# Expert rows added in memory by the DMA, and the attention's value product in two column halves

## What is computed

```python
out = jnp.einsum('bkgnqs,bnskd->bnqkgd', p.astype(v.dtype), vv)      # 8 heads share 2 value heads of 64
...
def hierarchical_moe(xn, ...):
    # every token picks TOP_K = 2 of 32 experts; gates = softmax over the two, times the group's weight
    order = jnp.argsort(expert_idx)                       # 2048 assignments, sorted by expert
    padded = (counts + 128 - 1) // 128 * 128              # each expert's rows are padded to blocks of 128
    x_pad = zeros.at[dest].set(xt[token_idx[order]])
    def expert_block(args):
        hb = jax.nn.silu(xb @ w_g[e]) * (xb @ w_u[e])     # 1024 -> 512
        return hb @ w_d[e]                                # 512 -> 1024
    y = y_pad[dest] * gates[order][:, None]
    out = zeros.at[token_idx[order]].add(y)
...
x = x + hierarchical_moe(rms_norm(x, norm_ffn), ...)
return rms_norm(x, norm_final)
```

## Time and profile before

| | us |
|---|---|
| median of 3 runs | 2939.61 |
| the runs | 2932.75 to 2940.99 |
| the profiled execution, its own time | 2939.56 |
| its span in the profile | 2937.8 |
| TensorE busy | 2763.1 (94%) |
| mean granted TensorE clock | 0.972 |

### The profile page before, as it was taken

How to read it: one execution, slowest core, us unless ns; L and a number is a source line. 1 busy time by engine, 2 the same in 40 slices (tenths; PEclk the granted TensorE clock), 3 DMA queues, 4 the chain that set the end, 5 groups by cost and what they waited for, 6 DMA issues and landing times. The chain is left out here.

```text
span 2937.8 us, 38551 instructions
## 1 busy us (share of the span) xinstructions
PE 2763.1 (94%) x14688; PEld 2408.4 (82%) x14688; DVE 1679.8 (57%) x2116; ACT 1179.0 (40%) x1703; POOL 514.7 (18%) x299
## 2 busy tenths in 40 slices
PE   8989999999899999999998998889999899999993
PEld 7989999899789999988776888666777588888883
DVE  5356655462443343343434732674444899999997
ACT  4342333421311111122334212564433377777774
POOL 3000000002022122100110000002610144444441
PEclk9999999999999999999999999999999899999997
DMA  5342323343211111113313121112302599999996
GB/s 193 103 135 84 99 86 109 119 141 115 86 51 44 49 50 43 50 50 108 134 65 108 44 60 63 37 51 94 108 24 110 185 414 418 414 413 417 413 414 250
DMA packets 244300, 436.95 MB, mean 149 GB/s; under 512 B 21698, under 2 KB 180690, under 8 KB 218594
## 3 DMA queue, kind: packets, MB, share of 16 engines
q1 hardware_dynamic: 234690, 400.88, 37.8%
q0 software_dynamic: 9504, 34.61, 2.9%
HBM read 375.54 MB, written 59.90 MB: 148 GB/s over the span
## 5 line engine op out<-in xcount | busy, mean ns | idle before, releaser
L3547 DVE TENSOR_TENSOR k_w_lo<-k_raw,k_w_hi 128x2048 fp32r<-128x2048 f32 x192 | 433.6, 2289 | 34.4 <-ACT k_w_hi L3483 31.0
L3483 ACT CAST k_w_hi<-k_raw 128x2048 fp32r<-128x2048 f32 x192 | 363.0, 1911 | 64.7 <-PE bank L3401 41.7
L120 PE MATMUL bank<-u_ffn_hi,f_w_hi 128*128 128x342 f32 (+1 forms) x840 | 292.3, 348 | 5.6 <-POOL f_w_lo L1362 5.6
L122 PE MATMUL bank<-u_ffn_hi,f_w_lo 128*128 128x342 f32 (+1 forms) x840 | 293.0, 349 | 0.0
L121 PE MATMUL bank<-u_ffn_lo,f_w_hi 128*128 128x342 f32 (+1 forms) x840 | 292.9, 349 | 0.0
L120 PE MATMUL bank<-u_hi,p_w_hi 128*128 128x342 f32 (+2 forms) x720 | 238.2, 331 | 8.9 <-DVEq L889 6.0
L121 PE MATMUL bank<-u_lo,p_w_hi 128*128 128x342 f32 (+2 forms) x720 | 232.4, 323 | 0.0
L122 PE MATMUL bank<-u_hi,p_w_lo 128*128 128x342 f32 (+2 forms) x720 | 231.9, 322 | 0.0
L3399 PE MATMUL bank<-k_w_hi,k_x_hi 128*128 128x512 f32 x512 | 203.1, 397 | 1.2 <-DVE k_x_lo L3553 1.0
L3401 PE MATMUL bank<-k_w_hi,k_x_lo 128*128 128x512 f32 x512 | 199.8, 390 | 0.0
L3400 PE MATMUL bank<-k_w_lo,k_x_hi 128*128 128x512 f32 x512 | 199.4, 389 | 0.0
(11 more groups left out here) (578 smaller groups left out, 6623.0 us busy)
## 6 DMA issues: line engine op xcount, KB each, us to landing
k_raw<-in_w_e_gate_dram SPq DMA_DIRECT2D x64, 1024.0 KB, 7.0
k_raw<-in_w_e_up_dram SPq DMA_DIRECT2D x64, 1024.0 KB, 7.5
k_raw<-in_w_e_down_dram SPq DMA_DIRECT2D x64, 1024.0 KB, 8.0
d_raw<-in_ffn_w_down_dram SPq DMA_DIRECT2D x44, 512.0 KB, 3.4
p_w<-in_w_in_dram SPq DMA_DIRECT2D x34, 512.0 KB, 4.3
f_raw<-in_ffn_w_gate_dram SPq DMA_DIRECT2D x22, 512.0 KB, 3.6
f_raw<-in_ffn_w_up_dram SPq DMA_DIRECT2D x22, 512.0 KB, 3.6
gate_scratch<-g_out SPq DMA_DIRECT2D x20, 513.0 KB, 6.3
```

The source lines that it names most:

```text
L120: pe.matmul(out, wh[:, t, :], xh[t][:, c:c + n], start=t == 0, stop=False)
L122: m = pe.matmul(out, wl[:, t, :], xh[t][:, c:c + n], start=False, stop=t == tiles - 1)
L3483: act.copy(wh[:, q, :], raw[:, r, :]).then_inc(hi_made, 1)
L3547: dve.tensor_tensor(wl[:, q, :], raw[:, r, :], wh[:, q, :], ALU.subtract).then_inc(lo_made, 1)
```

## The change

- `weigh`: no widened copy. Each value head's 64 columns are the weights of products that write to their own half of the output partitions, and products of the two halves now alternate. There are still four products of 512 columns a block, now with 64 weight columns instead of 128. GpSimd's three instructions and their semaphore are gone.
- Router: SyncE also stores the token rows `h` themselves to a new scratch tensor `sum_scratch`, 8 stores of 512 KB in runs of 512 bytes, among the stores of the normed rows. The gates go through the list of rows as a second column group: two more VectorE instructions, products of 96 columns instead of 48, and one more copy to `weight`.
- Experts: `gated` multiplies by the row's gate in the same instruction. The scatter adds its rows to `sum_scratch` in memory (`compute_op=ALU.add`), at the token's row; padding slots go to 128 spare rows. From the third on, gathers take their row numbers from `assigned` with a bound, so that padding slots, whose number is beyond it, are left out.
- End: one load of 512 KB a block, no adding on VectorE, and the norm on whole rows.

```diff
 # stage_mixers
-            pool.memset(vz[:, :, :, :], 0.0).then_inc(v_wide, 1)
-            pool.wait_ge(v_wide, 1)
-            for kv in range(2):
-                half = slice(kv * DH, (kv + 1) * DH)
-                pool.tensor_copy(vz[:, :, kv, half], va[:, :, half]).then_inc(v_wide, 1)
...
             def weigh(n):
-                if n == 0:
-                    pe.wait_ge(v_wide, 3)
                 pe.wait_ge(pt_kept, 4 * n + 4)
-                for kv in range(2):
-                    for r in range(2):
+                for r in range(2):
+                    for kv in range(2):
+                        half = slice(kv * DH, (kv + 1) * DH)
                         probs = pt[:, r, :, :].rearrange("p (g e) t -> p e g t", e=2)[:, kv]
-                        m = pe.matmul(T[1][:, :], vz[:, n + r, kv, :], probs, start=kv == r == 0, stop=kv == r == 1)
+                        m = pe.matmul(T[1][half, :], va[:, n + r, half], probs, start=r == 0, stop=r == 1)
 # stage_route
+            def rows_out(n):
+                sp.wait_ge(x_kept, n + 1)
+                if n in SHARED:
+                    sp.wait_ge(x_half, SHARED.index(n) + 1)
+                sp.dma_start(sum_d[n * P:(n + 1) * P, :].rearrange("p (k t) -> p k t", t=P), rows_of(h, n)).then_inc(h_stored, 16)
             for n in range(NB):
+                if n < NB - 2:
+                    rows_out(n)
+                if n == NB - 3:
+                    rows_out(NB - 2)
+                    rows_out(NB - 1)
                 sp.wait_ge(xn_made, n + 1)
                 sp.dma_start(xn_d[n * P:(n + 1) * P, :], xn[:, n % 4, :]).then_inc(stored[n % 4], 16)
...
+            sp.wait_ge(h_stored, 16 * NB)
...
-                m = pe.matmul(bank[7][:, 0:MAXB], at_place[:, c, :], in_block[:, c, :], start=c == 0, stop=c == 2 * NB - 1)
+                m = pe.matmul(bank[7][:, 0:2 * MAXB], at_place[:, c, :], in_block[:, c, :, :], start=c == 0, stop=c == 2 * NB - 1)
...
-                then(dve.tensor_tensor(in_block[:, half, :], *marks(begin[:, half], MAXB, begins[:, :]), ALU.is_equal))
-                return dve.tensor_tensor(in_block[:, half, :], in_block[:, half, :], own[:, half].unsqueeze(2).to_broadcast([P, NB, MAXB]), ALU.mult)
+                then(dve.tensor_tensor(in_block[:, half, 0, :], *marks(begin[:, half], MAXB, begins[:, :]), ALU.is_equal))
+                then(dve.tensor_tensor(in_block[:, half, 1, :], in_block[:, half, 0, :], gates[:, half].unsqueeze(2).to_broadcast([P, NB, MAXB]), ALU.mult))
+                return dve.tensor_tensor(in_block[:, half, 0, :], in_block[:, half, 0, :], own[:, half].unsqueeze(2).to_broadcast([P, NB, MAXB]), ALU.mult)
...
+            then(dve.tensor_copy(weight[:, 0:MAXB], bank[7][:, MAXB:2 * MAXB]))
 # stage_experts
+                    d = pool.indirect_dma_start(out=xg[:, s, :], out_offset=None, in_=xn_d, in_offset=rows_at, bounds_check=SEQ - 1, oob_is_err=False)
...
-                pool.indirect_dma_start(out=y_d, out_offset=bass.IndirectOffsetOnAxis(ap=to[:, s:s + 1], axis=0),
-                                        in_=y[:, s, :], in_offset=None).then_inc(stored[s], 16)
+                pool.indirect_dma_start(out=sum_d, out_offset=bass.IndirectOffsetOnAxis(ap=to[:, s:s + 1], axis=0),
+                                        in_=y[:, s, :], in_offset=None, compute_op=ALU.add).then_inc(stored[s], 16)
...
-                dve.tensor_tensor(hb[:, :].rearrange("p (k q) -> p q k", k=KE), sg[:, :].rearrange("p (q k) -> p q k", k=KE),
-                                  bank[3][:, :].rearrange("p (q k) -> p q k", k=KE), ALU.mult).then_inc(hb_made, 1)
+                dve.scalar_tensor_tensor(hb[:, :].rearrange("p (k q) -> p q k", k=KE), sg[:, :].rearrange("p (q k) -> p q k", k=KE), weight[:, ds(b, 1)],
+                                         bank[3][:, :].rearrange("p (q k) -> p q k", k=KE), ALU.mult, ALU.mult).then_inc(hb_made, 1)
...
             for b in range(NB):
-                if b >= RAW:
-                    sp.wait_ge(mixed, b - RAW + 1)
-                for j in range(2):
-                    sp.dma_start(raw[:, b % RAW, j * D:(j + 1) * D], y_d[j * SEQ + b * P:j * SEQ + (b + 1) * P, :]).then_inc(loaded[b % RAW], 16)
+                sp.dma_start(total[:, b, :], sum_d[b * P:(b + 1) * P, :]).then_inc(loaded[b], 16)
...
-                dve.scalar_tensor_tensor(rows_of(h, b), made(0, b), gates[:, b:b + 1], rows_of(h, b), ALU.mult, ALU.add).then_inc(first, 1)
-                dve.wait_ge(first, b + 1)
-                dve.scalar_tensor_tensor(rows_of(h, b), made(1, b), gates[:, NB + b:NB + b + 1], rows_of(h, b), ALU.mult, ALU.add).then_inc(mixed, 1)
-                if b:
-                    norm(b - 1)
-            norm(NB - 1)
```

More of the change, by code:

```diff
@@ L2023, in stage_mixers @@
 def stage_mixers(nc, ctx, A, K, bank, qa, ka, va, qk, vm, og, cols, dist, sinks, rows_d, mk, mv, mem_rows, w_in):
-    (scored, logit, maxed, exped, root, turned, pt_kept, pvmm, small, spread, inverse_kept, scaled, sq_made, sums, logs, rstd_made, placed, v_wide) = sems(
-        ctx, nc, "a", "scored logit maxed exped root turned pt_kept pvmm small spread inverse_kept scaled sq_made sums logs rstd_made placed v_wide")
+    (scored, logit, maxed, exped, root, turned, pt_kept, pvmm, small, spread, inverse_kept, scaled, sq_made, sums, logs, rstd_made, placed) = sems(
+        ctx, nc, "a", "scored logit maxed exped root turned pt_kept pvmm small spread inverse_kept scaled sq_made sums logs rstd_made placed")
     (bc0, bc1, rm_made, dec, gate_made, fmm, s_made, q_made, kt, kw_made, omm, den_made, hmade, umm, state,
@@ L2971, in rows_of, with stage_route @@
     return h[:, :, b * P:(b + 1) * P]
-def stage_route(nc, ctx, A, K, bank, h, gates, assigned, token, table, xn_d, wr, br, gain, raw, pieces_in):
-    (turned, x_kept, x_half, lmm, squared, roots, xn_made, stored_a, stored_b, stored_c, stored_d, rmm, cnt, iotas, rows, act_rows, marked, weighed, listed, lt_kept, l_turned) = sems(
-        ctx, nc, "r", "turned x_kept x_half lmm squared roots xn_made stored_a stored_b stored_c stored_d rmm cnt iotas rows act_rows marked weighed listed lt_kept l_turned")
+def stage_route(nc, ctx, A, K, bank, h, weight, assigned, token, table, xn_d, sum_d, wr, br, gain, raw, pieces_in):
+    (turned, x_kept, x_half, lmm, squared, roots, xn_made, stored_a, stored_b, stored_c, stored_d, rmm, cnt, iotas, rows, act_rows, marked, weighed, listed, lt_kept, l_turned, h_stored) = sems(
+        ctx, nc, "r", "turned x_kept x_half lmm squared roots xn_made stored_a stored_b stored_c stored_d rmm cnt iotas rows act_rows marked weighed listed lt_kept l_turned h_stored")
     ident, ones, eps, lower = (K[n] for n in ("ident", "ones", "eps", "lower"))
@@ L3249, in _ @@
             dve.tensor_copy(table[:, :], tf[:, :])
-            then(dve.memset(assigned[:, MAXB:MAXB + 2], 0))
+            then(dve.memset(assigned[:, MAXB:MAXB + 2], SEQ))
             dve.wait_ge(listed, 1)
@@ L3264, in stage_experts @@
     gathered, stored = (g0, g1), (s0, s1)
-    all_stored, gain_in, first, mixed, squared, normed, out_stored = sems(ctx, nc, "o2", "all_stored gain_in first mixed squared normed out_stored")
-    loaded = sems(ctx, nc, "o2", " ".join(f"in{r}" for r in range(RAW)))
+    all_stored, gain_in, squared, logs, rooted, normed, out_stored = sems(ctx, nc, "o2", "all_stored gain_in squared logs rooted normed out_stored")
+    loaded = sems(ctx, nc, "o2", " ".join(f"in{b}" for b in range(NB)))
     ident, eps = K["ident"], K["eps"]
@@ L3287, in tiles @@
             return ap.rearrange("p (k t) -> p k t", t=P)
[L3289 to L3294, removed]
+        total = h[:, :, :].rearrange("p k t -> p (k t)").rearrange("p (b d) -> p b d", d=D)
         def turn_of(j):
@@ L3343, in index, with gather @@
                 pool.wait_ge(index_made, g)
-            def gather(g, b, s):
-                index(g, from_, s, token, b)
+            def gather(g, b, s, whole=False):
+                index(g, from_, s, token if whole else assigned, b)
                 pool.sem_inc(waited, 1)
                 pool.wait_ge(waited, 1)
-                pool.indirect_dma_start(out=xg[:, s, :], out_offset=None, in_=xn_d,
-                                        in_offset=bass.IndirectOffsetOnAxis(ap=from_[:, s:s + 1], axis=0)).then_inc(gathered[s], 16)
+                rows_at = bass.IndirectOffsetOnAxis(ap=from_[:, s:s + 1], axis=0)
+                if whole:
+                    d = pool.indirect_dma_start(out=xg[:, s, :], out_offset=None, in_=xn_d, in_offset=rows_at)
+                else:
+                    d = pool.indirect_dma_start(out=xg[:, s, :], out_offset=None, in_=xn_d, in_offset=rows_at, bounds_check=SEQ - 1, oob_is_err=False)
+                d.then_inc(gathered[s], 16)
             def scatter(g, b, s):
@@ L3363, in end @@
                 pool.sem_inc(y_stored, 1)
-            gather(1, 0, 0)
-            gather(2, 1, 1)
+            gather(1, 0, 0, True)
+            gather(2, 1, 1, True)
```

(14 more changed lines are left out.)

34 lines of the change are left out of this document (17 added, 17 removed).

## The result

The changed kernel takes 2951.26 us (median of 6 runs, 2949.30 to 2954.14), the kernel before beside it 2940.85. The ratio is 1.0043, with an interval of 1.0025 to 1.0060: **slower**, by about 10 us (0.4%), where I had forecast 16 us less. The profiled execution took 2949.32 us with a span of 2947.6, against 2937.8 of before. I cut both spans at two points: the first row turn of the expert loop (TensorE turns a block's gathered rows) and the last scatter.

What follows compares the result with a forecast made beforehand. The expert loop was taken as bound by TensorE at 17.71 us a period, with DMA nearly touching and taking over after the change. Mixers -15.5, router +2.5, end -16.0, loop +13.4 sum to -15.6: 2924 us from 2939.56, range 2908 to 2952.

Steps and rivals of the forecast that it cites:

- Gathers leave out half of the slots: Expert loop: bounded gathers skip 2048 of 4096 slots, saving 0.64 us of DMA work a period if skipped rows cost nothing.
- case 4: Expert loop: left-out rows still take engine time, adding scatter at two plain ones; loop +32.6 us, total 2943; chance 0.08.
- My own sign of being wrong: Expert loop: main step wrong if the period stays at 17.71 us (near 2910) or exceeds 18.8 (slower than before).
- case 3: Expert loop: the adding scatter costs more than 2.4 plain ones, engines held during the read; at 3, 2962 us; chance 0.20.
- The adding scatter at two plain ones: Expert loop: a scatter that adds takes 2.58 us of DMA time, twice the plain 1.29, so +1.29 a period.
- The DMA work of 17.63 us: Expert loop before the change: DMA engines' work per period, from shrinking landing times, 0.08 us under TensorE's 17.71.
- 13.4: Expert loop: us added over 30 periods, 19.5 of extra DMA work less 6.1 of spare.
- When it sets in: Expert loop: extra DMA work reaches TensorE from about the fifth period, the period then going from 17.7 to 18.2-18.4 us.
- Mixers: `weigh`: passes in alternate column halves pair, 3.5 us becoming 1.75 a block; gain 15.5 us in all, lower end 0.
- Router: Router stage: added VectorE instructions +1.4 us and eight stores +1.1 us, together +2.5 us.
- the stores' term: Router: SyncE's eight added stores delay the stores of normed rows that VectorE waits for, +1.1 us, between 0 and 4.
- The end: After the last scatter: smaller first load, no VectorE adding, ScalarE leading with squares 1.75 us apart; -16.0 us, -12 to -17.

Runs made afterwards that it cites:

- e7: The changed kernel with each expert's rows seated evenly over the partitions instead of filling them from partition 0: 2928.69 us, ratio 0.9963 to the kernel before.
- e8: The changed kernel with the scatter bounded too, leaving out padding rows, and the rows seated evenly over the partitions: 2917.72 us, ratio 0.9934 to the kernel before.
- e2: The changed kernel with a plain scatter in place of the adding one: 2916.61 us, ratio 0.9919 to the kernel before.
- e4: The changed kernel with a bound on the scatter too, so its padding rows are left out: 2942.72 us, ratio 1.0019 to the kernel before.
- e9: The changed kernel with whole gathers and two plain scatters to scratch tensors in place of the adding one: 2944.26 us, ratio 1.0015 to the kernel before.
- e3: The changed kernel with all gathers whole, so padding slots are read as well: 2947.07 us, ratio 1.0023 to the kernel before.

## Why the prediction was wrong

- **The failed step: "Gathers leave out half of the slots: -0.64 us a period, if a left-out row costs nothing."** That left-out rows cost nothing held: e7 shows nearly this saving when it falls evenly (18.57 to 18.00, 0.57). What failed is the unspoken half of the step, that a saving in bytes is a saving on every engine. The rows lie on one side of the partitions, some engines save nothing, and a weight piece waits for those. Instead of -0.64 the term was 19.13 - 18.57 = +0.56, wrong by 1.2 us a period. That it isn't negative is explained by the seats; why it is above zero stays open. My case 4 had the saving at zero for another reason, and with it 2943; a loss was not among my bounds. My own sign of being wrong, a period beyond 18.8, came true.
- **Luck.** 2951 lies just inside my range of 2908 to 2952, but only because the range reached up into case 3, a dearer adding scatter, and that case is false.
- **The adding scatter at two plain ones** was right (18.57 beside 18.58). With this agrees the rule that the Trainium skill (Collectives: The Full Stack, on the bandwidth ceiling of a ring step) states, a reducing step at twice the time of a copying one. Case 3, more than 2.4 plain ones, falls: the outcome lies on its side of the forecast, but not by its mechanism.
- **The DMA work of 17.63 us** was 17.31. I took the fall of the landing times from 9.0 to 7.2 for a queue that was worked off at a steady rate. It was near its floor early: in the same view of before, the up pieces took 7.7 us from 2450 to 2550, 7.5 in the next 100 us, 7.2 after that and 7.2 at the end. Nor did the DMA share of 1.01 say that the engines were full, since e8 has it too, with room to spare. The error in the work hid part of the first one: 17.63 + 1.29 + 0.56 would be 19.48, above the measured 19.13. With 17.31 and even seats the sum is 17.31 - 0.64 + 1.27 = 17.94, close to e7's 18.00. In e7 the stretch from the first row turn to the last scatter took 584.9 us, 8.3 more than before, where I had 13.4.
- **When it sets in:** I expected the fifth block; it was the eleventh to twelfth.
- **Mixers** -15.5 forecast, -11 measured (12.3 in `weigh`, 1.3 lost behind it). The pairing was right; it is 1.94 and not 1.75 us at full clock, and up to 3.68 in the blocks at the lower level, of which there were four and not three as in the earlier trace rows.
- **Router** +2.5 forecast, +1.2 measured. From the first load to the list of rows in float (`r_list_float`) it is 57.6 us before (to 2309.71 in the earlier trace rows, from this row) and 58.8 after:

```profile
2252.16 0.80 SPq L3022 DMA_DIRECT2D k_raw<-in_w_e_gate_dram  x2
```

```profile
2241.35 0.81 SPq L3016 DMA_DIRECT2D k_raw<-in_w_e_gate_dram  x2
...
2300.14 0.27 DVE L3259 TENSOR_SCALAR r_list_float<-bank,r_spare 128x48 f32<-128x48 f32 x1
```

  The +1.2 are VectorE's added instructions: from the logits (2279.55 before, 2268.80 after) to this list it takes 30.2 and 31.3 us. The eight stores did cost something too: VectorE now waits 2.2 us for the stores of normed rows that free its buffers, and before it did not.

```profile
2264.22 1.97 DVE L3138 SCALAR_TENSOR_TENSOR r_xn<-qk,r_ss,r_gain 128x1024 f32<-128x1024 f32 x1 [1.40 <-DMA xn_scratch<-r_xn]
2266.99 1.97 DVE L3138 SCALAR_TENSOR_TENSOR r_xn<-qk,r_ss,r_gain 128x1024 f32<-128x1024 f32 x1 [0.80 <-DMA xn_scratch<-r_xn]
```

  It is hidden in the sum, because in this profile VectorE had waited 2.4 us less for TensorE ahead of it (7.2 instead of 9.6 us). So the stores' term was 2.2 and not 1.1, and only by chance is it missing from the total.
- **The end** -16.0 forecast, -12.3 measured. Mis-sized: the first load goes out 2.8 us later behind an adding scatter and not 0.6 (6.3 us, where a plain one took 3.4 before and 3.8 in e2; 0.6 of it is its longer issue on GpSimd, 1.58 instead of 0.98 us, and the rest was not taken apart). From the last norm to the end it takes 7.1 us where I took over 4.9, and the first load 3.8 instead of 3.4. The squares, 1.60 instead of 1.75 apart, gave 1.2 back.

## What to carry to other kernels

Before leaving out rows of a DMA, ask which engine they belong to: only what is saved on the fullest engine counts, since a transfer that needs all 16 waits for that one. If the padding stands at one end, seat the rows so that each group of partitions that one engine serves has its share; here a changed table in one comparison turned +0.4% into -0.4%, and with the scatter bounded too into -0.7%. When a profile calls the DMA engines full, look at engine time for a megabyte in a queue whose packets haven't changed: where it stands above its lowest (2.39 us here, up to 2.62), engines have room in it; what they wait for it doesn't tell. And read a period only from a stretch in which the same thing sets the pace throughout: e7's 17.88 was six periods of 17.71 and nine of 18.00.

## What the hardware showed that I had not expected

- The DMA share of a window stays at 1.00 when the engines have room: 386 GB/s in e8, whose loop goes by TensorE, 365 in e4 and 423 in e9 all stand beside shares of 1.00 to 1.02. (The 395 of e3 against the 423 of e9 is another matter: the rate counts an adding packet's bytes once.)
- Leaving out half of the rows made a DMA-bound loop slower than moving all of them, 19.13 against 18.57 us, as soon as the rows were uneven.
- Two products in alternate column halves pair though they stream different probabilities: 1.94 us where one after the other took 3.60.
